# Norm and rotary steps of a block's heads, taken in pairs instead of one by one

## The reference, cut to what matters

```python
h = rms_norm(x, norm1_g);  z = h @ w_in                  # 512 tokens
q, ks, kw = (rope(rms_norm(u, gain), pos) for u in heads_of_z)     # every head: norm over 64, then rotary
k_cmp, v_cmp = compress(kc), compress(vc)                # gelu(blocks @ w1) @ w2; k_cmp normed and rotated too
y_nsa = g0*softmax(q k_cmp) v_cmp + g1*softmax(q ks) vs + g2*softmax(q kw) vw     # "sparse" attention
qg, kg = rope(rms_norm(dil_q)), rope(rms_norm(dil_k))    # three groups, 12 heads more in pairs of 64 rows
y_dil = combine(dilated attention of the three groups)
merged = sigmoid(mg0)*(y_nsa @ w_up_nsa) + sigmoid(mg1)*(y_dil @ w_up_dil)
```

## Time and profile before

| what | value |
|---|---|
| median of three runs | 4267.94 us (4264.43 to 4272.28) |
| the profiled execution | 4260.17 us, span of its instructions 4258.9 us |
| TensorE busy | 3960.3 us, 93% of the span |
| VectorE, ScalarE, GpSimd busy | 50%, 36%, 12% |
| TensorE in the chain that ended last | 81% of the span |
| mean granted TensorE clock | 0.967 of full speed |

### The profile page before, as it was taken

The page is one execution under the profiler, slowest core; times in us unless marked ns, Lnnn a source line. Parts: engine busy times, 40 slices in busy tenths (PEclk is TensorE's granted clock), DMA queues, the critical chain, the costliest instruction groups (busy, mean ns, idle before and its releaser), DMA issues.

```text
span 4258.9 us, 47684 instructions
## 1 busy us (share of the span) xinstructions
PE 3960.3 (93%) x19722; PEld 3121.6 (73%) x19722; DVE 2141.2 (50%) x3752; ACT 1541.9 (36%) x1894; POOL 494.2 (12%) x748
## 2 busy tenths in 40 slices
PE   6988899999899889988798999999998999999999
PEld 4754778888665568866586877878877788888887
DVE  2275343333538344453353344778874566654444
ACT  3255432121334542234554333344444322222222
POOL 0000000000000000000001000166566111100000
PEclk8999999999999999999899999999999999999999
DMA  5400123332120012221112332354455656643332
GB/s 190 165 11 0 60 79 119 119 111 88 40 82 1 30 69 99 89 105 63 52 43 96 111 106 93 127 168 152 155 178 169 197 187 184 193 139 128 109 120 88
DMA packets 109833, 459.76 MB, mean 108 GB/s; under 512 B 9216, under 2 KB 43120, under 8 KB 68912
## 3 DMA queue, kind: packets, MB, share of 16 engines
q1 hardware_dynamic: 82048, 354.96, 23.9%
q0 software_dynamic: 27568, 101.74, 8.1%
HBM read 389.04 MB, written 67.63 MB: 107 GB/s over the span
## 4 chain that ended last, share of the span: by engine, by line
PE 81%; DVE 7%; ACT 5%; DMA 2%; POOL 2%; issue 2%; SPq 0%; DVEq 0%; ACTq 0%; POOLq 0%
PE ps L554 22%; PE ps L556 22%; PE ps L555 22%; PE ps L2308 2%; PE ps L981 1%; DVE ACC L1194 1%; PE ps L634 1%; POOL Y L2444 1%; PE ps L476 1%; DVE MX L1167 1%; PE ps L1061 1%; DMA stage<-in_w_mod 1%; DVE TD L711 1%; DMA gdram<-GST 1%; PE ps L1856 1%
## 5 line engine op out<-in xcount | busy, mean ns | idle before, releaser
L554 PE MATMUL ps<-HH,WH 128*128 128x512 f32 x2760 | 1062.6, 385 | 56.4 <-DVE HL L675 37.8
L555 PE MATMUL ps<-HL,WH 128*128 128x512 f32 x2760 | 1051.7, 381 | 0.0
L556 PE MATMUL ps<-HH,WL 128*128 128x512 f32 x2760 | 1051.0, 381 | 0.0
L447 DVE TENSOR_TENSOR WL<-stage,WH 128x2048 fp32r<-128x2048 f32 x248 | 567.8, 2290 | 481.9 <-ACT WH L436 481.9
L436 ACT ACTIVATE WH<-stage 128x2048 fp32r<-128x2048 f32 x248 | 472.8, 1907 | 587.1 <-PE ps L556 540.8
L554 PEld LDWEIGHTS ps<-HH,WH 128*128 128x128 f32 x2760 | 526.2, 191 | 169.9 <-issue 52.5
L556 PEld LDWEIGHTS ps<-HH,WL 128*128 128x128 f32 x2760 | 526.7, 191 | 106.5
L555 PEld LDWEIGHTS ps<-HL,WH 128*128 128x128 f32 x2760 | 526.0, 191 | 103.4 <-issue 0.7
L554 PE MATMUL ps<-AHp,WH 128*128 128x512 f32 x1024 | 407.0, 397 | 7.0 <-ACT Y L2626 7.0
L556 PE MATMUL ps<-AHp,WL 128*128 128x512 f32 x1024 | 406.6, 397 | 0.0
L555 PE MATMUL ps<-ALp,WH 128*128 128x512 f32 x1024 | 406.6, 397 | 0.0
(11 more groups left out here) (364 smaller groups left out, 4992.4 us busy)
## 6 DMA issues: line engine op xcount, KB each, us to landing
stage<-in_w SPq DMA_DIRECT2D x64, 1024.0 KB, 4.8
stage<-in_u SPq DMA_DIRECT2D x64, 1024.0 KB, 4.9
stage<-in_v SPq DMA_DIRECT2D x64, 1024.0 KB, 4.9
stage<-in_w_mod SPq DMA_DIRECT2D x48, 1024.0 KB, 4.9
GR<-gdram POOLq DMA_DIRECT2D x32, 1024.0 KB, 8.3
adram<-GR SPq DMA_DIRECT2D x22, 1024.0 KB, 4.1
AR<-adram POOLq DMA_DIRECT2D x88, 256.0 KB, 3.4
gdram<-GST SPq DMA_DIRECT2D x16, 1024.0 KB, 5.8
```

Of the source, the lines that this page charges most:

```text
L447: dve.e.tensor_tensor(k.WL[o % 2][:, 0:w], k.stage[n % 2][:, 0:w], k.WH[o % 2][:, 0:w].bitcast(F32), ALU.subtract).then_inc(*dve.done("sla ...
L554: pe.e.matmul(o, wh[:, kk, cs], L.hh[:, kk, z], start=first, stop=False)
L555: pe.e.matmul(o, wh[:, kk, cs], L.hl[:, kk, z], start=False, stop=False)
L556: mm = pe.e.matmul(o, wl[:, kk, cs], L.hh[:, kk, z], start=False, stop=last)
```

## The change

- Steps 2 and 3 are done for two heads at once. Behind an even chunk i: step 2 of heads i-2 and i-1; behind an odd one: step 3 of heads i-3 and i-2.
- ScalarE copies a chunk out first, then takes the roots of the pair (Ln, Ln, Exp, Exp), then squares the new head, from its copy in SBUF. A chunk's PSUM is free after the copy.
- The steps of the last pair of a set lie among the first two value tiles: step 2 behind tile 0, step 3 behind tile 1. On ScalarE the roots stand ahead of the sparse pieces of tile 0.
- hp 0 has one sparse piece per chunk instead of two, hp 1 two behind every chunk. So 6 pieces lie in the chunks of hp 0, 16 in its tiles, 12 in the chunks of hp 1 and two in its first value tile.
- `OB` has four buffers, with both `td`. In the last stage ScalarE now waits for the stores of heads 4 and 5 (OB0, OB1), and VectorE, ahead of zeroing `KD`, for those of the values of hp 1 (in `td`).

```diff
-    k.ob = [new(f"OB{i}", [128, 512])[:, :] for i in range(2)] + [k.td[0][:, 0:512]]
+    k.ob = [new(f"OB{i}", [128, 512])[:, :] for i in range(2)] + [t[:, 0:512] for t in k.td]
...
-    return [(j, step) for j, step in ((i - 2, 3), (i - 1, 2), (i, 1)) if 0 <= j < n]
+    return [(j, 2 if i % 2 == 0 else 3) for j in ((i - 2, i - 1) if i % 2 == 0 else (i - 3, i - 2)) if 0 <= j < n]
...
-def scalar_rope(k, act, key, step, src):
+def scalar_rope_raw(k, act, key, src):
+    if key[0] not in ("q", "kc"):
+        k.OB.take(act, key, out_end(key))
+    act.e.activation(head_rows(k, key), src, ACT.Copy).then_inc(*act.done("rope_raw", key))
+
+
+def scalar_rope_square(k, act, key):
     n = 31 if key[0] == "kc" else 512
...
+    t = k.TA.take(act, key, ("bones", key))
+    act.wait_ge("rope_raw", key)
+    act.e.activation(t[:, 0:n], head_rows(k, key), ACT.Square).then_inc(*act.done("rope_sq", key))
+
+
+def scalar_rope_roots(k, act, keys):
+
+    n = 31 if keys and keys[0][0] == "kc" else 512
+    for key in keys:
         r, p = k.RS.take(act, key, ("rope_add", key)), k.psn.of(("bones", key))
         act.wait_ge("bones", key)
         act.e.activation(r[:, 0:n], p[:, 0:n], ACT.Ln, bias=k.epsc[:, 0:1], scale=1.0 / 64).then_inc(*act.done("rope_ln", key))
+    for key in keys:
+        r = k.RS.of(key)
         act.wait_ge("rope_ln", key)
         act.e.activation(r[:, 0:n], r[:, 0:n], ACT.Exp, scale=-0.5).then_inc(*act.done("rope_rstd", key))
...
-    return lambda c: [("rope_sq", d_head(hp, c))]
+    return lambda c: [("rope_raw", d_head(hp, c))]
...
-            for _ in range(2 if c != 5 else 1):
+            for _ in range(1 + hp):
                 tensor_nsa(k, pe, next(nsa, []))
-        for i in (6, 7):
-            for j, step in rope_steps(i):
-                tensor_rope(k, pe, d_head(hp, j), step)
+        last = [6, 7]
         for name, v, tiles in d_values(hp):
             for tt in tensor_tokens(k, pe, name, 0, 0, 256, tiles, N1_READY, lambda tt, v=v: [("dv", (v, tt))], True):
+                for j, step in rope_steps(last.pop(0)) if last else []:
+                    tensor_rope(k, pe, d_head(hp, j), step)
...
-    act.wait_ge(*out_end(("dv", 1, 0)))
-    act.wait_ge(*out_end(("dv", 1, 1)))
+    act.wait_ge(*out_end(d_head(1, 4)))
+    act.wait_ge(*out_end(d_head(1, 5)))
...
-    dve.wait_ge(*out_end(d_head(1, 5)))
+    dve.wait_ge(*out_end(("dv", 1, 0)))
+    dve.wait_ge(*out_end(("dv", 1, 1)))
```

More of the change, by code:

```diff
@@ L1408, in out_end @@
 def out_end(key):
-    return ("rope_add", key) if key[0] in ("ks", "kw") else (f"ob{out_turn(key) % 3}", key)
+    return ("rope_add", key) if key[0] in ("ks", "kw") else (f"ob{out_turn(key) % 4}", key)
 def head_gain(k, key):
@@ L1447, in tensor_rope @@
         pe.e.matmul(p[:, 0:n], k.rotN[:, :], head_rows(k, key), start=True, stop=True).then_inc(*pe.done("rot2", key))
-def scalar_rope(k, act, key, step, src):
-    n = 31 if key[0] == "kc" else 512
-    if step == 1:
-        t = k.TA.take(act, key, ("bones", key))
-        if key[0] not in ("q", "kc"):
-            k.OB.take(act, key, out_end(key))
-        act.e.activation(head_rows(k, key), src, ACT.Copy).then_inc(*act.done("rope_raw", key))
-        act.e.activation(t[:, 0:n], src, ACT.Square).then_inc(*act.done("rope_sq", key))
-    elif step == 2:
+def scalar_rope_raw(k, act, key, src):
[3 more added lines that the diff above has]
+def scalar_rope_square(k, act, key):
+    n = 31 if key[0] == "kc" else 512
+    t = k.TA.take(act, key, ("bones", key))
[4 more added lines that the diff above has]
+    for key in keys:
         r, p = k.RS.take(act, key, ("rope_add", key)), k.psn.of(("bones", key))
@@ L1517, in z2_ends @@
 def z2_ends(c):
-    return [("kvc", c)] if c < 2 else [("rope_sq", N_HEADS[c - 2])]
+    return [("kvc", c)] if c < 2 else [("rope_raw", N_HEADS[c - 2])]
 def z2_linear(k):
@@ L1552, in tensor_heads @@
     for tt in tensor_tokens(k, pe, "v2a", 0, 0, 256, NAT, N1_READY, lambda tt: [("vsw", tt)], True):
-        for j, step in rope_steps(6 + tt):
+        for j, step in rope_steps(6 + tt) if tt < 2 else []:
             tensor_rope(k, pe, N_HEADS[j], step)
@@ L1574, in scalar_heads @@
             act.e.activation(k.KVC[:, c, :], p[:, 0:512], ACT.Copy).then_inc(*act.done("kvc", c))
-        for j, step in rope_steps(c - 2) if c >= 2 else []:
-            if step == 1:
-                act.wait_ge("chunk", (L.name, c))
-                act.wait_ge(*N1_READY)
-            scalar_rope(k, act, N_HEADS[j], step, p[:, 0:512])
+        if c >= 2:
+            act.wait_ge("chunk", (L.name, c))
+            act.wait_ge(*N1_READY)
+            scalar_rope_raw(k, act, N_HEADS[c - 2], p[:, 0:512])
+            scalar_rope_roots(k, act, [N_HEADS[j] for j, step in rope_steps(c - 2) if step == 2])
+            scalar_rope_square(k, act, N_HEADS[c - 2])
         if c >= 5:
@@ L1583, in scalar_heads @@
     for tt in range(4):
-        for j, step in rope_steps(6 + tt):
-            scalar_rope(k, act, N_HEADS[j], step, None)
+        if tt == 0:
+            scalar_rope_roots(k, act, [N_HEADS[j] for j, step in rope_steps(6)])
         act.wait_ge("chunk", ("v2a", 0, tt))
@@ L1686, in scalar_compress @@
             act.wait_ge("kz", 0)
-        scalar_rope(k, act, ("kc",), i - 3, k.kz[:, 0:31])
+            scalar_rope_raw(k, act, ("kc",), k.kz[:, 0:31])
+            scalar_rope_square(k, act, ("kc",))
+        elif i == 5:
+            scalar_rope_roots(k, act, [("kc",)])
 def vector_compress(k, dve, i):
@@ L1774, in scalar_dheads @@
         for c in scalar_linear(k, act, L):
-            for j, step in rope_steps(c):
-                if step == 1:
-                    act.wait_ge("chunk", (L.name, c))
-                scalar_rope(k, act, d_head(hp, j), step, k.psn.of((L.name, c))[:, 0:512])
-            for _ in range(2 if c != 5 else 1):
+            act.wait_ge("chunk", (L.name, c))
+            scalar_rope_raw(k, act, d_head(hp, c), k.psn.of((L.name, c))[:, 0:512])
+            scalar_rope_roots(k, act, [d_head(hp, j) for j, step in rope_steps(c) if step == 2])
+            scalar_rope_square(k, act, d_head(hp, c))
+            for _ in range(1 + hp):
                 scalar_nsa(k, act, next(nsa, []))
-        for i in (6, 7):
-            for j, step in rope_steps(i):
-                scalar_rope(k, act, d_head(hp, j), step, None)
+        last = [d_head(hp, j) for j, step in rope_steps(6)]
         for name, v, tiles in d_values(hp):
@@ L1792, in scalar_dheads @@
                                  ACT.Copy).then_inc(*act.done("dv", (v, tt)))
+                scalar_rope_roots(k, act, last)
+                last = []
                 for _ in range(2):
@@ L1805, in vector_dheads @@
                 vector_rope2(k, dve, d_head(hp, j), step)
-            for _ in range(2 if c != 5 else 1):
+            for _ in range(1 + hp):
                 vector_nsa(k, dve, next(nsa, []))
-        for i in (6, 7):
-            for j, step in rope_steps(i):
-                vector_rope2(k, dve, d_head(hp, j), step)
+        last = [6, 7]
         for name, v, tiles in d_values(hp):
@@ L1813, in vector_dheads @@
             for tt in range(4):
+                for j, step in rope_steps(last.pop(0)) if last else []:
+                    vector_rope2(k, dve, d_head(hp, j), step)
                 for _ in range(2):
```

## The result

| | median (runs) | profiled execution | its span | mean granted clock |
|---|---|---|---|---|
| before | 4266.2 us (4263.2 to 4272.3, four) | 4260.2 us | 4258.9 us | 0.967 |
| after | 4207.6 us (4204.4 to 4209.3, four) | 4206.1 us | 4204.8 us | 0.970 |

A forecast was written before the change was run, and what follows sets the result against it. TensorE, busy 93% of the span, bounds the kernel, so only its waits and lower clock, 77.5 us, can be won. Remaining 0.5 + 16.5 + 7.5 + 0 = 24.5, gain 53.0: 4267.9 - 53.0 = 4214.9, say 4215 us (4197 to 4241).

The forecast's parts named there:

- The likeliest case: Whole kernel: 24.5 of 77.5 us remain, gain 53.0, 4215 us; own bounds 4202 to 4228; chance 0.58.
- One cause: First set, hp 0 and hp 1: all TensorE waits come from queuing behind a head's roots with table loads, 4.8 us.
- A pair's roots: On ScalarE: 5.2 us against 7.7 for two singles, within TensorE's cover of 6.5 us plus a sparse piece.
- First set: Long product and transpose waits with clock, 14.1 us, go; 0.5 remains (0 to 2.5) at value tile 0's read-out.
- hp 0, value tiles: First value tiles of hp 0: 16.5 us remain (8 to 30): waits 7, 2, 1.3, 2.7, 1 and 2.5 for clock.
- hp 1: 7.5 us remain (4 to 14): 2 each at chunks 2 and 4, 2.7 at value tile 0, block turn 0.8.
- The clock: Lower TensorE clock behind waits: 4.3 us lost in first set, 16 hp 0, 3.8 hp 1; 2.5 left in hp 0.
- The gates: Stage behind the value tiles: zeroing 2.8 us later, a 1 us wait, taken back later; net 0 (-1 to +2.8).
- it doesn't do what it says: Rival: Ln and Exp share one table load, so pairs save less; gain about 45 us; no separate chance given.
- the clock: Rival, slower: from hp 0's tiles to hp 1 about 61 us more work at 1.2 GHz; 4277 us; chance 0.05.
- The drain: Rival: each table switch in a pair costs 1.4 us more, 2.8 in all; gain 32, 4236 us; chance 0.03.
- Better: Rival: ScalarE in time at hp 0's tile 0; 12 us or fewer remain, gain 66 or more; chance 0.08.

The follow-up runs named there:

- only_order: Kernel before with only ScalarE's chunk copy ahead of the roots and the square last, heads still one by one; 4246.1 us, ratio 0.9946.
- only_pieces: Kernel before with only the new spread of sparse pieces: one per chunk in hp 0, two in hp 1; 4239.3 us, ratio 0.9938.
- tile_copy_first: Kernel after with the first set's first value tile read out ahead of the last pair's roots; 4200.8 us, ratio 0.9843.
- last_pair_ahead: Kernel after with all steps of the last pair bare, ahead of the value tiles; 4209.7 us, ratio 0.9863.
- combined: Kernel after with the edits of `between` and `tile_copy_first` together; 4191.2 us, ratio 0.9824.
- unshared: Kernel after with Ln, Exp, Ln, Exp for a pair, so four table loads instead of two; 4229.7 us, ratio 0.9915.
- between: Kernel after with the first sparse piece ahead of the pair's steps on ScalarE and VectorE where two pieces follow; 4194.4 us, ratio 0.9834.
- last_store_apart: Kernel after with the last-stored output buffer in `BIG`, outside `td`, so VectorE's zeroing waits for the store before it; 4209.4 us, ratio 0.9861.

## Why the prediction was right

The forecast was 4215 (4197 to 4241), the result 4207.6. The likeliest case came true, and by the stages the forecast of both parts held: -15.1 for -13.6, -39.2 for -39.4. Two of these agreements are partly luck. The heads' total hides two errors of some 6 us each that cancel (below), and the 4206.1 us of the profile for 4207 needed 3.4 us more in code that wasn't changed. Step by step:

- **One cause.** The prediction put all waits of the earlier trace rows down to the roots with their table loads. For the first set `only_order` bears out that the read-out stood behind them. In hp 0 it was too much: in `only_pieces` the roots are as long as before, and the four waits between pieces (4.9, 4.0, 4.0, 3.2) are gone all the same, with 25.4 us of heads. One of them, 3.2, ends with VectorE's block score. Two of the seven, 3.3 and 4.9, lie at the bare last steps and not in the chunks.
- **A pair's roots.** 4.9 us measured for 5.2 (two Ln or Exp overlap a little). The cover held: no wait for VectorE's scaling in any chunk of hp 0 or hp 1. No drain is seen behind a load here either: Ln starts 0.01 us after it.
- **First set.** As forecast, the two waits went, and the clock was 1.00 at the long product. The read-out behind the roots grew from 3.9 to 4.2, where 0.5 more was the estimate. The stage gave 1.5 us more than forecast: TensorE's idle time fell by 9.6 (15.4 to 5.8) where 9.3 was forecast, and its busy time by 5.5 (92.1 to 86.5) where the clock had been priced at 4.3.
- **hp 0, chunks.** Nothing was left, as said.
- **hp 0, value tiles.** The wait of 7 is 6.4, for the block turn; 2 is 0.9; 2.7 is 2.4; 1.3 for small ones is 0.3; 1 for later block turns is 3.8 (0.9, 1.4 and 1.5, all in one tile). In sum that is 13.8 of waits for 14: the later tile's 3.8 for 1 is made good by the others. The reason was right: ScalarE's list shows the slab's high part starting at 2071.1, with the roots behind it, 2.6 us after the tile's last matmul (2068.5) where 4 had been taken, and the debt came from VectorE.
- **hp 1.** 2 each is 1.6 and 1.1; 2.7 is 2.1; the block turn 0.7 for 0.8. In sum 5.5 for 7.5.
- **The clock** is the term that was mis-sized. I left 2.5 us for it in hp 0 and nothing in hp 1. By the rows of the heads it still costs 0.05 x 240 = 12 us after the change, for 0.09 x 251 = 23 before, and TensorE's busy time for the same matmuls fell by 11.1 (251.5 to 240.4), where 16 + 3.8 - 2.5 = 17.3 was forecast. In its place the idle time of TensorE fell by 28.0 (48.2 to 20.1), for 43.6 - 21.5 = 22.1 forecast, since the rows that I summed held the long waits only: 4.6 us of idle time before were in none of them. The two errors, -6.2 and +5.9 us, cancel. That is why the heads came out as forecast, and it is luck.
- **The gates.** Zeroing starts 4.1 us behind the last tile for 1.2, 2.9 later (2.8 forecast), and TensorE waits 0.9 for the low part (1 forecast). `mg`'s store landed 32.0 us behind the tile, for 34.3 before, so not when it did but 2.3 earlier. The 3.3 us wait for the second dilated score became 0.2. With the new wait of 0.9 that makes 2.2 of the stage's 3.2 us, where I took 0. It is not a fixed gain: this wait is 1.6 and 2.0 in `tile_copy_first` and `last_pair_ahead` and 0.6 in `combined`, with the same code in this stage. But it is 2.2 or 3.3 in all five kernels with three buffers and 2.1 at most in the nine with four, so the fourth buffer may well have shortened it; why, no run shows.
- **The reasoning on sharing** was the weakest step. I wrote that ScalarE's 2.5 us per pair is by itself worth nothing and that what stands behind counts, but put no price on it. `unshared` gives the price: 22 us, at five waits of 2.8 or 2.9 each, a few small new ones and the clock behind them. It cost the forecast nothing only since the waits were worked out from the length of the pair. It did cost the rival "it doesn't do what it says", for which a gain of 45 was said, inside the first case: without shared loads the gain is 38.4 us (4268.1 to 4229.7), outside that case's own bounds.

Of the rivals, the clock came out in hp 0's tiles as described, but over 12 us of work and not 61. The drain was not seen. "Better" asked for ScalarE in time at tile 0. `between` reaches the 66 us or more that were said for it (70.9), but by another way: ScalarE is as late there, with the same wait of 5.0 us, and what TensorE needs stands ahead of the roots.

## What to carry to other kernels

An engine that is busy a third of the time can still set the pace by the length of one uninterrupted run on it: put what a faster engine needs next (the read-out that frees PSUM, the short transposed tile) ahead of the long run, not behind it. Batch only what gets shorter by it: pairs with shared table loads beat singles here, by 11 us with the new spread of the pieces, and pairs without them lost by 11 us to singles. When a wait is taken away, price the clock behind the waits that stay by the length of work that ran low behind like ones before, and look once more behind the last edit: moving a piece and a read-out ahead of the roots was worth 16 us on top of 59.

## What the runs showed that was not expected

The same code took different times in different executions, by more than the whole effect of some edits. The stretch ahead of the changed part took 1910.0 to 1920.0 us over fourteen profiled kernels, and the unchanged part behind took 1772.2 to 1782.2 us, while the medians of before on different chips agree to 2.7 us (4265.3 to 4268.1). Before and after alone differ by 6.9 us ahead of the changed part, against the change, and by 3.5 behind it, for it. Whether it is one kernel's layout or one execution's chance isn't settled: each kernel was profiled once. Comparing whole spans of two profiles is therefore good to some 10 us here. Stages cut at the same matmuls agree better: the first set is 92.3 to 92.4 us in the seven kernels that share it, the heads 258.4 to 260.6 in three that share them (after, `last_store_apart`, `tile_copy_first`), but the stage with the gates 155.7 to 158.6 in kernels with the same code there.

A table load had no drain behind it in any list read here: 1.28 us, and the next Ln or Exp 0.01 us later, as it was before the change.
